# A new order for the eleven product groups of an MLP block's second layer, and for the VectorE and ScalarE work behind them

## What is computed

```
h2 = rmsnorm(x, norm2_g[l]) * (1.0 + sc2) + sh2
x = x + gt2 * (jnp.square(jax.nn.relu(h2 @ w_ff1)) @ w_ff2)      # w_ff1 1024x4096, w_ff2 4096x1024
```

## Time and profile before

| what | us |
|---|---|
| median of 3 runs | 1175.83 |
| all runs | 1173.18, 1175.83, 1181.56 |
| the profiled execution | 1181.56 |
| its span, first to last instruction | 1179.8 |
| outside the span | 1.8 |

### The profile page before, as it was taken

The page is one execution under the profiler, slowest core; times in us unless marked ns, Lnnn a source line. Parts: engine busy times, 40 slices in busy tenths (PEclk is TensorE's granted clock), DMA queues, the critical chain, the costliest instruction groups (busy, mean ns, idle before and its releaser), DMA issues.

```text
span 1179.8 us, 19681 instructions
## 1 busy us (share of the span) xinstructions
PE 1130.3 (96%) x7237; PEld 1080.5 (92%) x7237; DVE 804.0 (68%) x1319; ACT 474.2 (40%) x780; POOL 347.1 (29%) x275
## 2 busy tenths in 40 slices
PE   5899999999989999999999999999999999999997
PEld 2698988898879999899999999999999999999996
DVE  5561455578775434678579879878788788798546
ACT  5551355545356344642233332432432423433431
POOL 0442111101434357764032032122121221230352
PEclk9999999999889999999999999999999999999998
DMA  8812523556523822111111112111101211111104
GB/s 312 314 60 89 152 82 130 185 161 211 174 84 118 267 92 73 54 55 36 37 36 55 54 37 72 53 36 53 60 29 59 65 32 60 50 53 54 37 1 144
DMA packets 67845, 109.85 MB, mean 93 GB/s; under 512 B 6434, under 2 KB 42566, under 8 KB 67398
## 3 DMA queue, kind: packets, MB, share of 16 engines
q1 hardware_dynamic: 57574, 84.88, 21.9%
q10 hardware_dynamic: 10208, 24.12, 6.6%
HBM read 96.81 MB, written 12.18 MB: 92 GB/s over the span
## 4 chain that ended last, share of the span: by engine, by line
PE 72%; DVE 15%; ACT 4%; issue 3%; DMA 3%; POOL 1%; SPq 1%; DVEq 0%; ACTq 0%; POOLq 0%
PE D L2404 6%; PE D L2406 6%; PE D L2405 6%; PE D L2588 6%; PE D L2590 5%; PE D L2589 5%; PE X L2588 5%; PE X L2590 5%; PE X L2589 5%; PE X L2660 4%; PE X L2662 3%; PE X L2661 3%; DMA RAWW<-in_WADA 2%; PE D L2662 2%; PE D L2660 2%
## 5 line engine op out<-in xcount | busy, mean ns | idle before, releaser
L2404 PE MATMUL D<-H_hi,W_hi 128*128 128x344 f32 x472 | 159.4, 338 | 3.7 <-POOL H_lo L1086 3.1
L1086 POOL TENSOR_TENSOR Y_lo<-FU,Y_hi 128x344 fp32r<-128x344 f32 (+3 forms) x84 | 105.3, 1257 | 168.5 <-ACT Y_hi L1519 90.4
L2405 PE MATMUL D<-H_lo,W_hi 128*128 128x344 f32 x472 | 153.0, 324 | 0.0
L2406 PE MATMUL D<-H_hi,W_lo 128*128 128x344 f32 x472 | 152.9, 324 | 0.0
L1081 POOL TENSOR_TENSOR W_lo<-RAWW,W_hi 128x1024 fp32r<-128x1024 f32 x25 | 61.7, 2469 | 185.6 <-ACT W_hi L1232 185.2
L2404 PEld LDWEIGHTS D<-H_hi,W_hi 128*128 128x128 f32 x472 | 91.1, 193 | 11.9 <-issue 7.6
L1086 POOL TENSOR_TENSOR Y_lo<-EY,Y_hi 128x344 fp32r<-128x344 f32 (+1 forms) x24 | 33.4, 1391 | 204.5 <-ACT Y_hi L1519 154.3
L2405 PEld LDWEIGHTS D<-H_lo,W_hi 128*128 128x128 f32 x472 | 90.9, 193 | 0.9 <-issue 0.5
L2406 PEld LDWEIGHTS D<-H_hi,W_lo 128*128 128x128 f32 x472 | 90.7, 192 | 0.0
L2212 DVE SCALAR_TENSOR_TENSOR X<-X,MOD 128x344 f32<-128x344 f32 (+1 forms) x138 | 75.6, 565 | 4.0 <-PE X L2662 3.8
L2014 DVE SCALAR_TENSOR_TENSOR X<-D,MOD,X 128x344 f32<-128x344 f32 (+1 forms) x72 | 41.3, 573 | 45.4 <-PE D L2590 24.6
(11 more groups left out here) (416 smaller groups left out, 3492.8 us busy)
## 6 DMA issues: line engine op xcount, KB each, us to landing
RAWW<-in_W SPq DMA_DIRECT2D x76, 512.0 KB, 3.5
RAWW<-in_WADA ACTq DMA_DIRECT2D x28, 512.0 KB, 4.3
RAWW<-in_WADA SPq DMA_DIRECT2D x20, 512.0 KB, 8.0
RAWW<-in_W ACTq DMA_DIRECT2D x18, 512.0 KB, 3.9
X0T<-in_x SPq DMA_DIRECT2D x3, 1376.0 KB, 12.5
out_y<-OUTN SPq DMA_DIRECT2D x24, 172.0 KB
X<-in_x SPq DMA_DIRECT2D x8, 344.0 KB, 5.8
NM<-nm_d SPq DMA_DIRECT2D x8, 256.0 KB, 5.6
```

What stands on the lines that cost most here:

```text
L1086: nc.gpsimd.tensor_tensor(lo_v, fu_v, hi_v.bitcast(F32), ALU.subtract).then_inc(lo_ready, 1)
L2404: T.matmul(out, w_h, hi[:, kt, a:b], start=(kt == 0), stop=False)
L2405: T.matmul(out, w_h, lo[:, kt, a:b], start=False, stop=False)
L2406: one = T.matmul(out, w_l, hi[:, kt, a:b], start=False, stop=(kt == KT - 1))
```

## The change

No operation is added or removed and no shape changes. These things change:

- TensorE's groups: S2 (onto M1's banks) moves ahead of A21, and A21 and A22 of chunk 2, once neighbours, are taken apart: S2, A21, S3, A22. The reading of chunk 2 (R2) comes after U2 and U3.
- All four T differences are put in chunk 0's columns (`T_PLACE`), T4 over T2, T1 over T3; they are free after U2 and U3.
- The cells of the weights (`F_CELL`) and the order of their splits follow. A1 of the next part no longer waits for M5 but for U3.
- VectorE: the sum S3 moves from behind M2's additions to ahead of T4 and R1's; `low(after, 0, "A1")` from behind M5's additions to behind R2's; S4's split from ahead of C21's additions to behind them.
- ScalarE: in `pair(b, 0)` the keep of A11 comes behind the high part of piece 0. A1's high part comes ahead of S4's.

```diff
-        T_PLACE = {"T2": (0, 0), "T3": (1, 0), "T4": (0, 2), "T1": (1, 2)}
+        T_PLACE = {"T1": 1, "T2": 0, "T3": 1, "T4": 0}
-        F_TILES = ("A11", "A12", "A21", "A22", "S2", "S3", "S1", "S4")
-        F_CELL = (1, 2, 0, 1, 2, 0, 2, 0)
+        F_TILES = ("A11", "A12", "S2", "A21", "S3", "A22", "S1", "S4")
+        F_CELL = (1, 2, 0, 1, 2, 0, 1, 0)
-        READS = ("M1", "R1", "M2", "R2", "U2", "U3", "C21", "M5", "M53")
+        READS = ("M1", "R1", "M2", "U2", "U3", "R2", "C21", "M5", "M53")
...
-                    last_of = {"A1": "M5", "S2": "M53", "S1": "M53", "S3": "C21", "A21": "C21"}[name]
+                    last_of = {"A1": "U3", "S2": "M53", "S1": "M53", "S3": "M5", "A21": "M5"}[name]
...
-                    read, p = {"A22": ("R1", 0), "S2": ("M2", 3), "S3": ("R2", 0), "S1": ("U2", 3), "S4": ("U3", 3)}[name]
+                    read, p = {"A21": ("R1", 0), "S3": ("M2", 3), "A22": ("U2", 3), "S1": ("U3", 0), "S4": ("C21", 3)}[name]
...
-                act.wait_ge(second_done, read_at(b, {"T2": "M1", "T3": "M2", "T4": "R2", "T1": "R2"}[name], PAIRS - 1))
+                act.wait_ge(second_done, read_at(b, {"T2": "M1", "T3": "M2", "T4": "U2", "T1": "U3"}[name], PAIRS - 1))
...
                 relu_piece(b, i, 0)
-                if i == 0:
-                    keep(b, i, "A11")
                 hi_piece(b, i, 0)
-                if i:
-                    keep(b, i, "A11")
+                keep(b, i, "A11")
...
                 hi_piece(b, 1, 5)
+                f_upper(b, "S2")
+                t_upper(b, "T2")
                 f_upper(b, "A21")
-                t_upper(b, "T2")
-                f_upper(b, "A22")
-                f_upper(b, "S2")
                 t_upper(b, "T3")
                 f_upper(b, "S3")
+                f_upper(b, "A22")
                 t_upper(b, "T4")
+                f_upper(b, "S1")
                 t_upper(b, "T1")
-                f_upper(b, "S1")
+                after = (b[0], b[1] + 1)
+                ring(after, 0, "A1")
                 f_upper(b, "S4")
-                after = (b[0], b[1] + 1)
-                for name in ("A1", "S2", "S1", "S3"):
+                for name in ("S2", "S1", "S3"):
                     ring(after, 0, name)
...
                 add_all(b, "M1")
-                f_lower(b, "A21")
+                f_lower(b, "S2")
+                f_sum(b, "S3")
                 t_add(b, "T4")
                 add_all(b, "R1")
-                f_lower(b, "A22")
+                f_lower(b, "A21")
                 add_all(b, "M2")
-                f_lower(b, "S2")
-                f_sum(b, "S3")
-                add_all(b, "R2")
                 f_lower(b, "S3")
                 add_all(b, "U2")
+                f_lower(b, "A22")
+                add_all(b, "U3")
                 f_lower(b, "S1")
-                add_all(b, "U3")
-                f_lower(b, "S4")
+                add_all(b, "R2")
+                low(after, 0, "A1")
                 dve.wait_ge(f_lo, f_at(b, "S1"))
                 sums_12(after, 0)
                 add_all(b, "C21")
+                f_lower(b, "S4")
                 add_all(b, "M5")
-                low(after, 0, "A1")
                 add_all(b, "M53")
```

On TensorE `second_seven` changes in the same sense:

```diff
+                weights_there(b, "S2")
+                split_there(b, "T2")
+                for p in every:
+                    read(b, "M1", p)
+                    second_part(A[p], "S2", p, 0, 0, start=False, onto=True).then_inc(second_done, 1)
                 weights_there(b, "A21")
                 for p in every:
                     read(b, "M2", p)
                     second_part(B[p], "A21", p, 0, 2, stop=False)
-                weights_there(b, "A22")
-                for p in every:
-                    second_part(B[p], "A22", p, 1, 2, start=False).then_inc(second_done, 1)
...
+                weights_there(b, "A22")
+                for p in every:
+                    second_part(B[p], "A22", p, 1, 2, start=False).then_inc(second_done, 1)
                 split_there(b, "T4")
                 for p in every:
                     read(b, "U3", p)
-                    second_part(A[p], "A22", p, 0, 2, start=False, onto=True).then_inc(second_done, 1)
+                    second_part(A[p], "A22", p, 0, 0, start=False, onto=True).then_inc(second_done, 1)
```

More of the change, by code:

```diff
@@ L730, in build @@
         T_CELL = {"T1": EY[:, KT:KT + 2, CH:2 * CH], "T2": FU[:, 2:4, 0:CH], "T3": EY[:, 0:2, CH:2 * CH], "T4": FU[:, 0:2, 0:CH]}
-        T_PLACE = {"T2": (0, 0), "T3": (1, 0), "T4": (0, 2), "T1": (1, 2)}
-        F_TILES = ("A11", "A12", "A21", "A22", "S2", "S3", "S1", "S4")
-        F_CELL = (1, 2, 0, 1, 2, 0, 2, 0)
+        T_PLACE = {"T1": 1, "T2": 0, "T3": 1, "T4": 0}
+        F_TILES = ("A11", "A12", "S2", "A21", "S3", "A22", "S1", "S4")
+        F_CELL = (1, 2, 0, 1, 2, 0, 1, 0)
         F_RAW = {"A21": 4, "A22": 5, "A11": 6, "A12": 7}
         F_SUMS = ("S1", "S2", "S4", "S3")
-        READS = ("M1", "R1", "M2", "R2", "U2", "U3", "C21", "M5", "M53")
+        F_ON_DVE = ("A11", "A12", "S4")
+        READS = ("M1", "R1", "M2", "U2", "U3", "R2", "C21", "M5", "M53")
         PAIRS = KT // 2
@@ L1155, in t_lower @@
             def t_lower(b, name):
-                lo(split_of(b, name), quadrant(Y_hi, *T_PLACE[name]), quadrant(Y_lo, *T_PLACE[name]), T_CELL[name])
+                i = T_PLACE[name]
+                lo(split_of(b, name), quadrant(Y_hi, i, 0), quadrant(Y_lo, i, 0), T_CELL[name])
             def twice_seven(b):
@@ L1547, in f_upper @@
                     act.wait_ge(d_full[1], direct_at(b, 1))
-                elif name == "A21":
+                elif name == "S2":
                     seven_there(act, b, 1, "A22")
@@ L1558, in t_upper @@
                 act.wait_ge(full_ready, full_of(b, name) + 1)
-                act.wait_ge(second_done, read_at(b, {"T2": "M1", "T3": "M2", "T4": "R2", "T1": "R2"}[name], PAIRS - 1))
-                nc.scalar.activation(quadrant(Y_hi, *T_PLACE[name]), T_CELL[name], ACT.Copy).then_inc(hi_ready, 1)
+                act.wait_ge(second_done, read_at(b, {"T2": "M1", "T3": "M2", "T4": "U2", "T1": "U3"}[name], PAIRS - 1))
+                nc.scalar.activation(quadrant(Y_hi, T_PLACE[name], 0), T_CELL[name], ACT.Copy).then_inc(hi_ready, 1)
             def pair(b, i):
@@ L2708, in second_seven @@
                     second_part(B[p], "A12", p, 1, 0).then_inc(second_done, 1)
-                weights_there(b, "A21")
-                for p in every:
-                    read(b, "M2", p)
-                    second_part(B[p], "A21", p, 0, 2, stop=False)
-                weights_there(b, "A22")
-                for p in every:
-                    second_part(B[p], "A22", p, 1, 2, start=False).then_inc(second_done, 1)
                 weights_there(b, "S2")
@@ L2720, in second_seven @@
                     second_part(A[p], "S2", p, 0, 0, start=False, onto=True).then_inc(second_done, 1)
+                weights_there(b, "A21")
+                for p in every:
+                    read(b, "M2", p)
+                    second_part(B[p], "A21", p, 0, 2, stop=False)
                 weights_there(b, "S3")
@@ L2733, in second_seven @@
                     read(b, "R2", p)
-                    second_part(B[p], "S1", p, 1, 2).then_inc(second_done, 1)
+                    second_part(B[p], "S1", p, 1, 0).then_inc(second_done, 1)
                 weights_there(b, "S4")
```

## The result

| | before | changed |
|---|---|---|
| median of 6 runs, us | 1178.35 | 1188.18 |
| lowest to highest | 1173.18 to 1181.56 | 1185.46 to 1190.19 |
| span of the profiled execution | 1179.8 | 1186.4 |

The changed kernel is slower: ratio 1.0092, 95% interval 1.007 to 1.0113, so 8 to 13 us: 10.8 by the ratio, which rests on more runs than the table, and 9.8 by the table's medians. The forecast was +9.9 and 1185.7 in all. The median of 1188.18 lies within the range of 1180 to 1193 and 2.5 above the forecast, which is as much as the median of the kernel before rose with three more runs (1175.83 to 1178.35).

A forecast was written before the change was run, and what follows sets the result against it. The prediction took the loop's rounds to be bound by TensorE, busy 99.86%. Its terms, +7.5 for the sum, +2.4 for the keep and 0 for the rest, gave 1175.83 + 9.9 = 1185.7 us, range 1180 to 1193.

The forecast's parts named there:

- the one stall per round: At M2's first matmul TensorE waits for VectorE's first addition of R1, losing 0.41 us per round, 2.4 us in all.
- not slower: Rival: M2's stall comes from the change of group or bank, so the insertion is absorbed; 1175.8 to 1173.5 us, chance 0.05.
- Part 1: VectorE's sum S3 ahead of R1 delays M2 by 1.25 us in six rounds: +7.5 us, bounds +7.5 and +15.7.
- the 1.21 with 0.04 to the next instruction: Price of the inserted VectorE sum, taken from the like instruction L2150 and the gap behind it: 1.25 us.
- GpSimd and the sum: GpSimd is idle at the sum S3's new place on VectorE, so the sum takes 1.21 us, not 2.57.
- the rival of 1193.9: GpSimd still slows the sum S3 to 2.57 us: 18.1 us more, 1.5% slower, chance 0.08.
- Part 2: ScalarE's later keep in pair 0 delays S2's first matmul, 4 x 0.49 + 2 x 0.2 = +2.4 us.
- the rival of 1183.3: The keep behind the first ScalarE split costs nothing, only the sum's +7.5 us stands; chance 0.15.
- Part 3: The new order of TensorE's eleven groups meets each wait in time: 0 us.
- S4's cover: VectorE finishes M5's first addition 0.45 us before S4's group needs it; failing rival 1189.3 us, chance 0.12.
- Part 4: SyncE's later reloads of tiles 0, 1 and 3 stay hidden by 2 us or more: 0 us.
- Within 1%: The whole kernel's time stays within 1% of before, chance 0.66; over 1% slower means above 1187.6 us.

The follow-up runs named there:

- s3_sum_back: The changed kernel with the sum S3 put back behind M2's additions; ratio to the kernel before 1.0003.
- r1_first: The changed kernel with the keep back and, on VectorE, T4 and R1's additions ahead of S2's weight split and the sum S3; ratio to the kernel before 1.0.
- before_r1_first: The kernel before with A21's weight split moved behind R1's additions, nothing else; ratio to the kernel before 0.9995.
- before_keep: The kernel before with only the keep of A11 in pair 0 moved behind the high part; ratio to the kernel before 1.0023.
- both_back: The changed kernel with both the sum S3 and the keep put back, leaving the new order of groups; ratio to the kernel before 0.9996.
- keep_back: The changed kernel with the first keep of pair 0 back ahead of the high part; ratio to the kernel before 1.0074.
- cover_taken: both_back with one unused VectorE instruction of 0.68 us more per round, ahead of the sums for the next part; ratio to the kernel before 1.0031.
- t4_no_wait: The changed kernel with T4 ahead of the sum S3 and without VectorE's wait for its own sum S3; M2's step 1.60 us in the loop's rounds.

## Why the prediction was right, step by step

- *What bounds the kernel; the one stall per round* (0.41 at M2, from VectorE's addition of R1). Right: s3_sum_back, r1_first and before_r1_first move it up, down and away by moving VectorE's queue alone. The rival "not slower", in which M2's stall belonged to the group or bank, is refuted: r1_first keeps groups and banks and has no stall.
- *Part 1, the sum ahead of R1*, +7.5 us. The mechanism was right, the size 8.8 us: 1.48 per round instead of 1.25. The mis-sized term is "the 1.21 with 0.04 to the next instruction", 1.47 to 1.48 by the trace. It was read off L2150 and its follower, and no wait for a fresh result stands before L2150. In its new place the sum needs the split's result (0.12 more) and has a wait for its own result behind it (0.22 more than none), while without these it shifts its followers by 1.14 only. Nearer rows existed in the profile of before. A sum with a T difference behind it, like S3 and T4 now, is S4 and T3:

```profile
784.45 1.84 DVE L2153 TENSOR_TENSOR RAWW<-RAWW 128x1024 f32<-128x1024 f32 x1
786.42 0.88 DVE L2134 TENSOR_TENSOR EY<-FU,EY 128x688 f32<-128x688 f32 x1
```

T3 starts 0.13 behind the sum's drawn end, not 0.04. And the split overlapped its follower T4 by 0.07, which a follower that needs its result would lose, for a gap of 0.03. That makes 1.21 + 0.13 + 0.10 = 1.44, which is 0.03 short of the 1.47 measured.
- *GpSimd and the sum.* Right: 1.224 us, six of six, against the 2.57 of the earlier trace rows; with it falls the rival of 1193.9. The rule that the prediction takes from the Trainium skill, "SBUF — State Buffer", section "Who interferes with whom", held in both places.
- *Part 2, the keep*, +2.4 us. Right: 2.3 in the changed kernel, four large and two small, and 2.1 to 2.3 in five periods of before_keep and s3_sum_back, where it stands alone (2.18 over the kernel before, 2.10 over both_back). keep_back shows that it isn't hidden, so the rival of 1183.3 falls.
- *Part 3, the new order*, 0. Right: both_back. *S4's cover*: predicted 0.45, in the changed kernel the addition starts at 822.50 for 0.57, so ends at 823.07, and the group starts at 823.39, 0.32. Thinner, but it held; cover_taken shows that it was real and what it costs when it's gone, 0.43 a round.
- *Part 4, the loads*, 0. No wait for a load appears in TensorE's list; no run tried it further.
- *The sum.* 8.8 + 2.3 = 11.1 by the trace, 9.9 forecast, 10.8 by the ratio, 9.8 by the medians, with an interval of 8 to 13 that holds all of them. So the nearness of forecast and medians, 0.1 us, is partly luck: the trace says that part 1 was short by 1.3 us. "Within 1%" came true by a narrow margin: the interval of the ratio reaches 1.0113.

## What to carry to other kernels

Where an engine is busy over 99.8% of a loop, read its start times one by one before a reorder: the only wait of a round was invisible in the list of waits, and everything put ahead of the instruction that ends it is paid in full, in every round. Put first in a late engine's queue what another engine waits for next, and behind it what has a group's time to spare (in r1_first R1's additions took 2.3 us ahead of the split, and it was still done 1.7 us before its group). And price an inserted instruction by the distance between the starts of its neighbours in a like place with like waits, not by its length.

## What the runs showed of the hardware that was not expected

- Waiting for its own last result costs VectorE more than a wait should. With T4 behind the sum it is 0.20 us in the loop (1.35 against 1.15 from start to start) and 0.12 in the first round (1.26 against 1.14). Part of it is the lost overlap: without a wait the next instruction starts 0.07 to 0.08 us before the drawn end of its forerunner, so a 0.68 us instruction costs 0.60 (cover_taken) and a 1.21 one 1.14 (t4_no_wait). The rest grows in the loop with the number of waits that the follower has; that register instructions are the reason is argued, not shown.
- After a wait TensorE loses some 0.10 more on its second matmul. In nearly all such places here the first is drawn 0.42 or 0.43 long and the next starts 0.26 later instead of 0.16, whether the step before was 1.94 or 0.23; in a few it is drawn 0.40 and the next comes after 0.23 or 0.24. In before_r1_first the wait itself can't be seen (a step of 0.15) and the 0.26 is there all the same.
- The granted clock outside the rounds differs from one execution to the next. In the stretch of 300 to 400 us its mean was 0.93 of 2.4 GHz in the profiled execution of before and 0.97 in that of the changed kernel, though nothing there was changed:

```profile
300.00:400.00 100.00, 90.75 (x595) 83.73 (x595) 65.36 (x123) 50.48 (x78) 44.53 (x39) 0.93 0.43 134
```

```profile
300.00:400.00 100.00, 92.21 (x621) 85.14 (x620) 65.62 (x128) 51.01 (x80) 44.73 (x39) 0.97 0.47 147
```

The first row is of before, the second of the changed kernel. From 0 to 100 us it is the other way round, 1.00 and 0.91. The changed kernel was 1.49 us ahead where the five periods begin (656.38 against 657.87), and took 1.48 us less from their end to the end of the span (102.68 against 104.16, mean clock 0.97 against 0.95). These two are the difference between 6.6 us of spans and 9.57 us of five periods. How much of them is the clock wasn't worked out. TensorE was busy 91 to 92% in both stretches above; why the clock was lower in the one stays open.
